# Transposing attention probabilities by an fp32 product with a diagonal of the softmax factors, in place of scaling them in place and transposing

## The chip, the cores and the metric

The kernel runs on one core of one Trainium2 chip. The metric is the device time of one launch in microseconds. Before the change three runs took 1724.89, 1728.59 and 1732.99 us, so the median is 1728.59 us. Everything is float32: one sequence of 256 tokens with 1024 features goes through two blocks of two layers each, and every weight is read from HBM once.

## The reference, cut to what matters

The model holds four mixers with softmax attention. The change touches the softmax of all of them. For one head it is always this, with a causal or banded mask and sometimes a bias, a sink or a gate:

```
def forgetting_attention(q, k, v, f_logit, b_f):        # 8 heads
    logits = einsum('bqhd,bkhd->bhqk', q, k) * scale + c_q - c_k
    p = softmax(where(kpos <= qpos, logits, -inf), axis=-1)
    out = einsum('bhqk,bkhd->bqhd', p, v)

def mla_mixer(...):      # 8 heads:  the same, with rotated parts of q and k
def dilated_mixer(...):  # 12 heads in three groups of patterns; the softmax runs over the three together:
    o, lse = banded_attention(...)             # per pattern
    wts = softmax(stack(lses), axis=0); out = sum(wts * stack(outs))
def swa_mixer(...):      # 8 heads, a sink column in the softmax
def nsa_mixer(...):      # 8 heads, two attentions each (selected blocks, window), each times its own gate:
    out = gate[0] * o_cmp + gate[1] * o_slc + gate[2] * o_win
```

With e = exp(logits - max) the kernel computes p = e * f, where f is 1 / sum(e) for each query (times the gate where there is one). Queries lie on the partitions, so f is one number per partition. The product with v needs p with the keys on the partitions, so p must be transposed.

## The kernel before, in words

The program is one stream of stages over one core: input projections, mixers, output products and feed-forward networks, most of whose time is split-precision products (each float32 weight is split into a high and a low part by ScalarE and VectorE, lines 339 and 347, and TensorE makes three products of the parts, lines 718 to 720, and 939 and 940). The attentions run between an input projection and the output product of their layer, and the output product's parts are interleaved with them.

The class `Attention` (line 1171) writes one attention. The 256 queries are two tiles of 128 (t = 0, 1). A unit is one head; for t = 0 it needs 128 keys and for t = 1 all 256, so its probabilities are 384 columns on 128 partitions, in one of `homes`. Two units (j = 0, 1) make a duo; G duos make a pair m, over which the softmax factor is shared. G is 1 everywhere but in the dilated mixer, where it is 3. The attentions are: fox, 4 duos; mla, 4 duos; dilated, 2 pairs of 3 duos; and the last layer's (sliding window with sinks and the two branches of nsa), 12 duos. That makes 26 duos and 22 pairs. mla and dilated are chained by `Chain` (line 2693), the second starting 4 steps after the first, so that some steps hold work of both.

The order of work is written out by hand, step by step, and every engine executes its own queue in order. In step i:

- TensorE (`tensor`) makes `flips(d, 0)` of an earlier duo d, the `scores` of duo i, a half part of the output product in some steps, `flips(d, 1)`, the `values` of the duo flipped one step before, and the other half part. With G = 1 the duo flipped in step i is i - 2.
- VectorE (`vector`) copies the flip of j = 0 out of PSUM (line 1358), makes the factors of pair i - 1 where G is 1 (line 1352: a reciprocal of the row sums), then adds the bias to the scores of duo i and takes the negative row maxima (line 1326).
- ScalarE (`scalar`) copies the flip of j = 1 out of PSUM (line 1405) and makes the exponentials with their row sums (line 1397).
- GpSimd (`scale`, line 1430) waits for the factors, multiplies them by the gate where there is one (line 1425), and multiplies the probabilities in place, in 128x128 for t = 0 and 128x256 for t = 1, with one count of `pool_a` per unit.

`flips(d, j)` (line 1268) waits for GpSimd's count of its own unit and for the copy that empties the bank of the flip before it: all flips of an attention go through one PSUM bank. It then transposes three blocks of 128x128, `pe.transpose` with the identity as the moving operand (line 1274). The copies go to a ring of four duos, from which `values` (line 1294) multiplies with v. `add_bias` may overwrite a home of probabilities only after its flip (`probs_flipped`).

Of the kernel before, what the change touches and what calls it, by code (L numbers as in the profile page):

```python
# [10 lines left out]
ALU = mybir.AluOpType  # L11
# [1159 lines left out]
class Attention:  # L1171
# [3 lines left out]


    def __init__(self, k, ctx, pairs, first_tile, base=None, banks=(4, 5, 6, 7), started=(), values_in=None,
                 homes=None):
        self.k, self.pairs, self.first_tile = k, pairs, first_tile
        self.base = base or (lambda tile: None)  # L1180
        self.banks, self.started, self.values_in = banks, started, values_in
        self.at = Begun(k)
        self.M, self.G = len(pairs), len(pairs[0]["units"])
        self.duos = self.M * self.G
        self.LAG = 2 if self.G == 1 else 3
        self.DEPTH = len(homes) if homes else 8 if self.G == 1 else 12
        self.RING_T = 4
        self.steps = self.flip_step(self.duos - 1) + 3
        M, G = self.M, self.G

        def sb(name, shape):
            return ctx.enter_context(k.nc.sbuf_tensor(f"att{k.uid()}_{name}", shape, F32))

        if homes is None:
            probs = sb("probs", [P, self.DEPTH, 3 * P])
            homes = [probs[:, n, :] for n in range(self.DEPTH)]
        self.homes = homes
        self.probs_T = k.spare[:].rearrange("p r n -> p (r n)").rearrange("p (r j n) -> p r j n", r=self.RING_T, j=2)
        self.nmax_u, self.rows = sb("nmax_u", [P, M, 2, TT, G]), sb("rows", [P, M, 2, TT, G])
        self.nmax, self.den, self.fac, self.esink = (sb(n, [P, M, 2, TT]) for n in ("nmax", "den", "fac", "esink"))  # L1200

    def flip_step(self, d):

# [42 lines left out]
    def tensor(self, pe, i, between=None):  # L1246

        k = self.k

        def scores(d):  # L1250
            if d == 0:
                for mark in self.started:
                    pe.wait_ge(*mark)
            if d >= 1:
                pe.wait_ge(*self.at.logits_ready.after(2 * d))
            for t in range(TT):
                keys = P * (t + 1)
                for j in range(2):
                    x, out = self.unit(d, j), self.scores_bank(j)[:, self.spots(t)]
                    right = x["tiles"][:, 0:t + 1] if "tiles" in x else x["kT"][:, 0:keys]  # L1260
                    ins = pe.matmul(out, x["q"](t), right, start=True, stop="extra" not in x)  # L1261
                for j in range(2):
                    x, out = self.unit(d, j), self.scores_bank(j)[:, self.spots(t)]
                    for lhsT, rhs in x.get("extra", ()):
                        ins = pe.matmul(out, lhsT, rhs[:, 0:keys], start=False, stop=rhs is x["extra"][-1][1])
            ins.then_inc(self.at.scores_ready.sem, 1)

        def flips(d, j):
            n = 2 * d + j
            pe.wait_ge(*self.at.pool_a.after(n + 1))  # L1270
            if n >= 1:
                pe.wait_ge(*(self.at.probs_T_ready.after(d + 1) if j else self.at.act_a.after(d)))
            for c in range(3):
                ins = pe.transpose(self.flip_bank()[:, P * c:P * c + P], self.probs(n)[:, P * c:P * c + P],  # L1274
                                   k.ident[:])
            ins.then_inc(self.at.probs_flipped.sem, 1)

        def values(d):
            pair = self.pairs[d // self.G]
            tile = pair["tile"]  # L1280
            if d == 0 and self.values_in:
                pe.wait_ge(*self.values_in)
            opens = pair["first"] and d % self.G == 0
            if opens:
                if tile >= 1:
                    pe.wait_ge(*self.at.heads_done.after(tile))
                if self.base(tile):
                    pe.matmul(self.mixed(tile), *self.base(tile), start=True, stop=False, skip_group_check=True)
                    opens = False
            pe.wait_ge(*self.at.probs_T_ready.after(d + 1))  # L1290
            pe.wait_ge(*self.at.act_a.after(d + 1))
            for s in range(TT):
                for j in range(2):
                    ins = pe.matmul(self.mixed(tile)[HD * j:HD * j + HD, P * s:S], self.unit(d, j)["v"](s),  # L1294
                                    self.probs_T[:, d % self.RING_T, j, S * s:S + P * s], start=opens and s == 0,
                                    stop=s == 1 and self.closes(d), skip_group_check=True)
            ins.then_inc(self.at.heads_ready.sem, 1)

        d = self.duo_at(i)
        if d >= 0:  # L1300
            flips(d, 0)
        if i < self.duos:
            scores(i)
        if between:
            between()
        if d >= 0:
            flips(d, 1)
        d = self.duo_at(i - 1)
        if d >= 0:
            values(d)  # L1310
# [107 lines left out]
    def scale(self, pool):  # L1418

        k, G = self.k, self.G  # L1420
        for m in range(self.M):
            gate = self.pairs[m].get("gate")
            pool.wait_ge(*self.at.dve_a.after(m + 1))
            if gate is not None:
                k.pool.done(pool, pool.tensor_tensor(self.fac[:, m], self.fac[:, m], gate, ALU.mult))
            for g in range(G):
                for j in range(2):
                    for t in range(TT):
                        x = self.probs(2 * (m * G + g) + j)[:, self.spots(t)]
                        ins = pool.tensor_tensor(x, x, self.fac[:, m, j, t:t + 1].to_broadcast(list(x.shape)), ALU.mult)  # L1430
                    ins.then_inc(self.at.pool_a.sem, 1)

    def passed(self):

        k, duos, M = self.k, self.duos, self.M
        for mark, n in ((k.scores_ready, duos), (k.heads_ready, duos), (k.logits_ready, 2 * duos),
                        (k.probs_flipped, 2 * duos), (k.pool_a, 2 * duos), (k.probs_T_ready, duos), (k.act_a, duos),
                        (k.probs_ready, M), (k.dve_a, M), (k.dve_b, sum(not self.plain(m) for m in range(M)))):
            mark.passed(n)
        tiles = self.pairs[-1]["tile"] + 1  # L1440
        k.act_b.passed(tiles)
        k.heads_done.passed(tiles)
# [1285 lines left out]
def latent_layer(k, block, enter):  # L2728

    with ExitStack() as ctx:  # L2730
        z, bias = k.layer_views((TT, 2720), (12, S))
        ab = Latent(k, ctx, z, bias)
        ab.loads(block, k.acc[0])
        pieces = [("token", lambda t, c=c, n=n: z[:, t, c:c + n], n) for c, n in AB_CUTS]
        mla = Attention(k, ctx, [dict(tile=p, first=True, last=True, units=[(ab.head(2 * p), ab.head(2 * p + 1))])
                                 for p in range(ab.H // 2)], 0, banks=(4, 5, 6, 7),
                        started=(ab.head_placed.after(8),), values_in=ab.copied[-1], homes=ab.homes)
        product(k, block, "ab_in", KD, pieces, enter, scaled=True, side=ab, then=None)
        k.bias_loaded.passed(16)
        heads_out = k.heads_done.after(0)  # L2740
        mla.passed()
        dil = Attention(k, ctx, [dict(tile=p, first=True, last=True, units=[tuple(ab.dilated(4 * g + 2 * p + j)
                                                                                  for j in range(2)) for g in range(3)])
                                 for p in range(2)], NH, banks=(4, 5, 6, 7), started=(k.logits_ready.after(0),),
                        values_in=k.heads_done.after(0), homes=ab.wide_homes)
        out = OutProduct(k, "ab_out", 6)

        def tile_waits(pe, m):
            if m < 4:
                pe.wait_ge(heads_out[0], heads_out[1] + (2 if m < 2 else 4))  # L2750
            else:
                pe.wait_ge(*k.heads_done.after(2))

        attend(k, block, Chain(mla, dil, 4), out, {6: [0], 8: [1], 10: [2], 12: [3]}, {3: 4, 11: 5, 13: 6, 15: 8},
               side=ab, tile_waits=tile_waits)
        dil.passed()
        out.weights(block)
# [473 lines left out]
```

## Time and profile before

| | |
|---|---|
| median of 3 runs | 1728.59 us |
| the profiled execution | 1731.53 us, span 1729.8 us |
| mean granted TensorE clock | 0.973 of full |
| TensorE busy | 1646.2 us (95%), 8997 matmul records |
| VectorE, ScalarE, GpSimd busy | 1125.7, 942.9 and 117.3 us |
| HBM | 281.81 MB read, 164 GB/s over the span |

Durations in the profile are those of single instructions; matmuls are pipelined, so what one costs in a dense run is the distance between starts. The granted clock has two levels, 1.2 and 2.4 GHz (0.5 and 1.0). In a window that mixes them, PEclk is the mean. The attentions lie at about 122 to 158 us (fox), 945 to 1010 us (mla and dilated) and 1463 to 1528 us (the last layer's). The chain of waits names what each moment of the end time rests on; a line that isn't in it had time to spare at that place.

### The profile page before, as it was taken

How to read it: one execution, taken by the hardware profiler on the slowest of the kernel's cores; microseconds unless marked ns; L12 is line 12 of the kernel's file. 1: busy time of each engine (PE TensorE's matmuls, PEld its weight loads, DVE VectorE, ACT ScalarE, POOL GpSimd, SP SyncE). 2: the span in 40 equal slices, each digit the busy share in tenths (PEclk: the TensorE clock that was granted, in tenths of full speed). 3: DMA queues.
4: the chain of work that ended last, by engine and by line, in shares of the span. 5: the costliest groups of instructions: out<-in, count | busy, mean ns of one | idle time of the engine just before them, and what ended most of it. 6: DMA issues, size and time to landing. Idle time of an engine off the chain costs nothing.

```text
span 1729.8 us, 24635 instructions
## 1 busy us (share of the span) xinstructions
PE 1646.2 (95%) x8997; PEld 1384.6 (80%) x8997; DVE 1125.7 (65%) x1784; ACT 942.9 (55%) x1528; POOL 117.3 (7%) x172
## 2 busy tenths in 40 slices
PE   7998999989889998999999789999999998899998
PEld 7886888888678887888877568888888878578887
DVE  5955766677666667766667457666766673667665
ACT  5544655457565545555556555556555554665454
POOL 0601000000000000000003210000000010410000
PEclk9998999999999999999999899999999998999999
DMA  9332455574336554646464026645465673026652
GB/s 331 105 122 98 147 178 186 188 257 136 107 114 203 194 169 146 201 164 218 161 239 147 1 79 213 211 161 198 160 217 164 224 239 130 1 74 219 198 166 97
DMA packets 215698, 283.91 MB, mean 164 GB/s; under 512 B 8264, under 2 KB 151624, under 8 KB 215624
## 3 DMA queue, kind: packets, MB, share of 16 engines
q1 hardware_dynamic: 215624, 282.93, 48.8%
q8 instruction: 46, 0.75, 0.2%
q14 instruction: 28, 0.23, 0.0%
HBM read 281.81 MB, written 1.09 MB: 164 GB/s over the span
## 4 chain that ended last, share of the span: by engine, by line
PE 86%; DVE 7%; ACT 5%; issue 1%; POOL 1%; DMA 0%; ACTq 0%; SPq 0%; DVEq 0%
PE banks L939 28%; PE banks L940 14%; PE banks L718 12%; PE banks L720 12%; PE banks L719 12%; PE banks L1261 1%; DVE ring_lo L347 1%; PE banks L1294 1%; PE banks L1274 1%; ACT ring_hi L339 1%; PE banks L653 1%; PE banks L1622 1%; PE banks L2880 1%; ACT act_both L637 0%; DVE ffn_down_lo L1060 0%
## 5 line engine op out<-in xcount | busy, mean ns | idle before, releaser
L939 PE MATMUL banks<-act_both,ring_hi 128*128 128x512 f32 x2112 | 750.5, 396 | 3.3 <-DVE act_both L592 1.6
L940 PE MATMUL banks<-act_both,ring_lo 128*128 128x256 f32 x2112 | 592.1, 280 | 0.0
L939 PEld LDWEIGHTS banks<-act_both,ring_hi 128*128 128x128 f32 x2112 | 397.1, 188 | 100.7 <-issue 3.9
L940 PEld LDWEIGHTS banks<-act_both,ring_lo 128*128 128x128 f32 x2112 | 397.0, 188 | 5.0
L1055 DVE TENSOR_TENSOR ring_lo<-weight_slots,ring_hi 128x1024 fp32r<-128x1024 f32 x240 | 283.3, 1222 | 62.2 <-ACT ring_hi L1010 61.8
L347 DVE TENSOR_TENSOR ring_lo<-weight_slots,ring_hi 128x1024 fp32r<-128x1024 f32 (+4 forms) x150 | 181.9, 1227 | 97.0 <-ACT ring_hi L339 93.8
L1010 ACT ACTIVATE ring_hi<-weight_slots 128x1024 fp32r<-128x1024 f32 x240 | 239.2, 1044 | 0.8 <-DMA weight_slots<-in_ffn_w 0.7
L1024 ACT ACTIVATE normed<-banks 128x512 f32<-128x512 f32 x132 | 78.9, 598 | 286.3 <-PE banks L940 286.3
L718 PE MATMUL banks<-ffn_down_hi,ffn_hidden_hi 128*128 128x512 f32 x528 | 207.5, 393 | 0.3
L719 PE MATMUL banks<-ffn_down_lo,ffn_hidden_hi 128*128 128x512 f32 x528 | 206.7, 392 | 0.0
L720 PE MATMUL banks<-ffn_down_hi,ffn_hidden_lo 128*128 128x512 f32 x528 | 205.9, 390 | 0.0
L339 ACT ACTIVATE ring_hi<-weight_slots 128x1024 fp32r<-128x1024 f32 (+4 forms) x150 | 145.8, 992 | 91.4 <-PE banks L720 86.0
L1060 DVE TENSOR_TENSOR ffn_down_lo<-weight_slots,ffn_down_hi 128x1024 fp32r<-128x1024 f32 x132 | 160.8, 1218 | 3.1 <-ACT ffn_down_hi L1017 3.1
L718 PE MATMUL banks<-ring_hi,act_both 128*128 128x512 f32 (+3 forms) x360 | 147.3, 409 | 6.4 <-DVE act_both L2240 1.9
L720 PE MATMUL banks<-ring_hi,act_both 128*128 128x512 f32 (+3 forms) x360 | 139.8, 388 | 0.0
L719 PE MATMUL banks<-ring_lo,act_both 128*128 128x512 f32 (+3 forms) x360 | 139.6, 388 | 0.0
L1017 ACT ACTIVATE ffn_down_hi<-weight_slots 128x1024 fp32r<-128x1024 f32 x132 | 137.8, 1044 | 0.0
L1028 ACT ACTIVATE ffn_silu<-normed 128x256 f32<-128x256 f32 x132 | 55.2, 418 | 137.3 <-DVE normed L1077 95.2
L718 PEld LDWEIGHTS banks<-ffn_down_hi,ffn_hidden_hi 128*128 128x128 f32 x528 | 99.1, 188 | 25.5 <-DVE ffn_down_lo L1060 2.9
L720 PEld LDWEIGHTS banks<-ffn_down_hi,ffn_hidden_lo 128*128 128x128 f32 x528 | 99.2, 188 | 22.0
L1074 DVE TENSOR_TENSOR normed<-banks,normed 128x256 f32<-128x256 f32 x88 | 37.3, 424 | 115.1 <-ACT normed L1024 114.4
L719 PEld LDWEIGHTS banks<-ffn_down_lo,ffn_hidden_hi 128*128 128x128 f32 x528 | 99.1, 188 | 15.8
(378 smaller groups left out, 1925.6 us busy)
## 6 DMA issues: line engine op xcount, KB each, us to landing
weight_slots<-in_ffn_w SPq DMA_DIRECT2D x44, 1024.0 KB, 6.4
weight_slots<-in_ffn_w_gate SPq DMA_DIRECT2D x44, 1024.0 KB, 5.4
weight_slots<-in_ffn_w_up SPq DMA_DIRECT2D x44, 1024.0 KB, 8.0
weight_slots<-in_ffn_w_down SPq DMA_DIRECT2D x88, 512.0 KB, 8.4
weight_slots<-in_ffn_w SPq DMA_DIRECT2D x44, 512.0 KB, 8.3
weight_slots<-in_ev_w_in SPq DMA_DIRECT2D x6, 2048.0 KB, 12.8
weight_slots<-in_od_w_in SPq DMA_DIRECT2D x5, 2048.0 KB, 10.6
weight_slots<-in_ab_w_in SPq DMA_DIRECT2D x4, 2048.0 KB, 11.0
```

The lines of the kernel that those rows point to most:

```text
L339: act.activation(self.hi(n), part.raw, ACT.Copy).then_inc(self.part_hi, 1)
L347: dve.tensor_tensor(self.lo(n), part.raw, self.hi(n).bitcast(F32), ALU.subtract).then_inc(self.part_split, 1)
L718: pe.matmul(out, left[0], right[0], start=start, stop=False, **more)
L719: pe.matmul(out, left[0], right[1], start=False, stop=False, **more)
L720: return pe.matmul(out, left[1], right[0], start=False, stop=stop, **more)
L939: pe.matmul(bank, k.hi(n)[:, q, :], k.act_both[:, q], start=q == 0, stop=False, skip_group_check=True)
L940: return pe.matmul(bank[:, 0:S], k.lo(n)[:, q, :], k.act_hi[:, q, :], start=False, stop=q == KD - 1, skip_group_check=True)
L1010: act.activation(k.hi(part(f, u)), k.parts[part(f, u)].raw, ACT.Copy).then_inc(k.part_hi, 1)
L1017: act.activation(dn_hi[:, f % 2], raw_down(f), ACT.Copy).then_inc(k.down_hi.sem, 1)
L1024: act.activation(cross[:, f % 2], ps[:, bank:bank + 2, S:2 * S], ACT.Copy).then_inc(k.cross_copied.sem, 1)
L1055: dve.tensor_tensor(k.lo(n), k.parts[n].raw, k.hi(n).bitcast(F32), ALU.subtract).then_inc(k.part_split, 1)
L1060: dve.tensor_tensor(dn_lo[:, f % 2], raw_down(f), dn_hi[:, f % 2].bitcast(F32), ALU.subtract).then_inc(k.down_split.sem, 1)
```

## The change

The probabilities stay unscaled. GpSimd builds, per pair m, unit j and query tile t, a diagonal matrix of 128x128: the identity times the factors, broadcast along the row. TensorE multiplies each block of probabilities with the diagonal of its query tile by an ordinary fp32 `matmul` (probabilities stationary, diagonal moving) in place of `transpose` with the identity: the result is the scaled transpose. There are two sets of diagonals (m % 2), so GpSimd waits for the flips of pair m - 2 before it writes; the dilated attention uses the storage of mla's, and waits for all of mla's flips. `pool_a` counts two per pair, not two per duo. The row sums (`den`) are now written to the storage of the factors, and the reciprocal is made in place.

```diff
@@ Attention.__init__
-        self.nmax, self.den, self.fac, self.esink = (sb(n, [P, M, 2, TT]) for n in ("nmax", "den", "fac", "esink"))
+        self.nmax, self.fac, self.esink = (sb(n, [P, M, 2, TT]) for n in ("nmax", "fac", "esink"))
+        self.den = self.fac
+        self.diag = sb("diag", [P, 2, 2, TT, P]) if diag is None else diag
+        self.shared = diag is not None
@@ flips
         def flips(d, j):
-            n = 2 * d + j
-            pe.wait_ge(*self.at.pool_a.after(n + 1))
+            n, m = 2 * d + j, d // self.G
+            pe.wait_ge(*self.at.pool_a.after(2 * m + j + 1))
             if n >= 1:
                 pe.wait_ge(*(self.at.probs_T_ready.after(d + 1) if j else self.at.act_a.after(d)))
             for c in range(3):
-                ins = pe.transpose(self.flip_bank()[:, P * c:P * c + P], self.probs(n)[:, P * c:P * c + P],
-                                   k.ident[:])
+                ins = pe.matmul(self.flip_bank()[:, P * c:P * c + P], self.probs(n)[:, P * c:P * c + P],
+                                self.diag[:, m % 2, j, min(c, 1), :], start=True, stop=True, skip_group_check=True)
             ins.then_inc(self.at.probs_flipped.sem, 1)
@@ scale
-            for g in range(G):
-                for j in range(2):
-                    for t in range(TT):
-                        x = self.probs(2 * (m * G + g) + j)[:, self.spots(t)]
-                        ins = pool.tensor_tensor(x, x, self.fac[:, m, j, t:t + 1].to_broadcast(list(x.shape)), ALU.mult)
-                    ins.then_inc(self.at.pool_a.sem, 1)
+            if m >= 2 or self.shared:
+                pool.wait_ge(*self.at.probs_flipped.after(2 * G * max(m - 1, 0)))
+            for j in range(2):
+                for t in range(TT):
+                    ins = pool.tensor_tensor(self.diag[:, m % 2, j, t, :], k.ident[:],
+                                             self.fac[:, m, j, t:t + 1].to_broadcast([P, P]), ALU.mult)
+                ins.then_inc(self.at.pool_a.sem, 1)
@@ passed
-                        (k.probs_flipped, 2 * duos), (k.pool_a, 2 * duos), (k.probs_T_ready, duos), (k.act_a, duos),
+                        (k.probs_flipped, 2 * duos), (k.pool_a, 2 * M), (k.probs_T_ready, duos), (k.act_a, duos),
@@ latent_layer
-                        values_in=k.heads_done.after(0), homes=ab.wide_homes)
+                        values_in=k.heads_done.after(0), homes=ab.wide_homes, diag=mla.diag)
```

## Rows read from the trace of the kernel before

**Rows 1.** Page: span, busy time and share of each engine, chain of waits by engine.
```profile
span 1729.8 us, 24635 instructions
...
PE 1646.2 (95%) x8997; PEld 1384.6 (80%) x8997; DVE 1125.7 (65%) x1784; ACT 942.9 (55%) x1528; POOL 117.3 (7%) x172
...
PE 86%; DVE 7%; ACT 5%; issue 1%; POOL 1%; DMA 0%; ACTq 0%; SPq 0%; DVEq 0%
```

**Rows 2.** Windows (us): busy and count of PE, PEld, DVE, ACT, POOL; PEclk, DMA share, GB/s.
```profile
122.30:158.50 36.20, 34.67 (x165) 24.76 (x166) 14.79 (x51) 16.30 (x46) 8.49 (x16) 0.81 0.01 2
132.50:135.90 3.40, 2.81 (x20) 1.92 (x19) 1.67 (x9) 0.83 (x3) 1.90 (x4) 1.00 0.00 0
135.90:146.20 10.30, 10.21 (x37) 6.97 (x38) 3.10 (x13) 3.43 (x16) 1.90 (x4) 0.50 0.01 2
945.00:1010.00 65.00, 48.94 (x279) 33.66 (x278) 25.64 (x110) 30.96 (x106) 19.84 (x40) 0.84 0.11 34
996.10:999.50 3.40, 3.33 (x15) 2.30 (x16) 0.29 (x2) 1.44 (x2) 3.11 (x7) 0.50 0.00 0
1463.00:1490.80 27.80, 18.28 (x136) 12.93 (x134) 21.40 (x95) 17.16 (x63) 9.84 (x20) 0.88 0.21 72
1490.80:1528.50 37.70, 36.90 (x236) 25.48 (x238) 20.64 (x74) 21.73 (x72) 19.55 (x37) 1.00 0.12 36
```

**Rows 3.** Line 1274 (transposes) in last attention: count, ns min/median/max, first and last start.
```profile
L1274 PE MATMUL banks<-ident,layer x72: 270/273/421, 1469.2 to 1525.4; 128*128 128x128 f32 x72
```

**Rows 4.** Line 1261 (scores), last attention, by form.
```profile
L1261 PE MATMUL banks<-cd_zT x96: 272/376/632, 1463.1 to 1517.4; 64*128 64x128 f32 x48, 64*128 64x256 f32 x48
```

**Rows 5.** Timeline of TensorE: start us, us, line, operands, count.
```profile
919.30 1.03 PE L2454 MATMUL banks<-ident,layer 128*128 128x128 f32 x8
920.09 0.47 PE L718 MATMUL banks<-ring_hi,act_both 128*128 128x512 f32 x1
...
43.10 1.95 PE L1622 MATMUL banks<-layer 128*128 128x128 f32 x16
44.80 0.48 PE L718 MATMUL banks<-ring_hi,act_both 128*128 128x512 f32 x1
...
687.85 0.61 PE L974 MATMUL banks<-diag_rrms,ones 128*128 128x128 f32 x4
```

**Rows 6.** Chain of waits in order of time: start us, us, what.
```profile
135.99 0.87 PE banks L1274 x3
...
143.78 0.64 PE banks L1274 x3
...
147.64 0.33 PE banks L1274 x3
...
950.46 0.98 POOL normed L1430 x2
...
967.15 0.87 PE banks L1274 x3
...
989.02 3.62 ACT ab_flipped L1397 x16
...
1493.87 0.33 PE banks L1274 x3
```

**Rows 7.** Groups by form (busy us, mean ns | idle) and a wait, in windows of the attentions.
```profile
L1430 POOL TENSOR_TENSOR ab_flipped<-ab_flipped,att_fac 128x128 f32<-128x128 f32 x10 | 4.0, 403 | 27.5 <-DVE att_fac L1352 27.5
L1430 POOL TENSOR_TENSOR ab_flipped<-ab_flipped,att_fac 128x256 f32<-128x256 f32 x10 | 6.2, 617 | 0.0
...
PE banks L1274 <- POOL layer L1430: 1.6, 2, 1.0
...
L347 DVE TENSOR_TENSOR ring_lo<-weight_slots,ring_hi 128x1024 fp32r<-128x1024 f32 x6 | 7.3, 1217 | 1.1 <-ACT ring_hi L339 1.1
L347 DVE TENSOR_TENSOR ring_lo<-weight_slots,ring_hi 128x1024 fp32r<-128x1024 f32 x8 | 11.0, 1376 | 3.2 <-ACT ring_hi L339 3.1
```

More of the change, by code:

```diff
@@ L1177, in __init__ @@
     def __init__(self, k, ctx, pairs, first_tile, base=None, banks=(4, 5, 6, 7), started=(), values_in=None,
-                 homes=None):
+                 homes=None, diag=None):
         self.k, self.pairs, self.first_tile = k, pairs, first_tile
```

## The prediction

> **What bounds the kernel now.** I read the page first. TensorE is busy 95% of the span and holds 86% of the chain of waits [rows 1]; whatever lengthens its instruction stream is paid unless it waits at that place for something else. So the question is how full TensorE is where the edited code runs. The windows of those stretches answer it [rows 2]. The last attention (the one with 12 pairs of heads) is solid from 1490.8 on: 36.90 us busy of 37.7, at full clock. The first attention (122.3 to 158.5) is as full, 34.67 of 36.2, but at a mean clock of 0.81. The two chained attentions (945 to 1010) have 48.94 of 65.0 at 0.84, and the start of the last one (1463 to 1490.8) has 18.28 of 27.8, where VectorE with 21.40 is the fuller. GpSimd is busy 8.5, 19.8, 9.8 and 19.6 us in the four and sets the pace in none. I call a flip the three transposes of one head's probabilities into the shared bank. There are 26 pairs of heads, so 52 flips.
>
> **What TensorE pays per flip.** Before, a flip is three records: the last attention has 12 pairs, 12 x 2 x 3 = 72, and the trace has 72 [rows 3]. An fp32 product is not one record but two: the scores of the same 12 pairs are 24 products over 128 keys and 24 over 256, and the trace has 48 and 48 [rows 4]. So a flip goes from three records to six. What a record costs is its pitch, not its duration of about 273 ns, because they are pipelined. Eight transposes start at 919.30 and the next instruction at 920.09, which is 0.10 each; within the run (1.03 - 0.27)/7 is 0.109. Sixteen records of 128x128 fp32 products start at 43.10, the next one at 44.80: 0.106 each, or (1.95 - 0.275)/15 = 0.112 within. Four records with a diagonal as moving operand are (0.61 - 0.274)/3 = 0.112 [rows 5]. I take 0.11 for both kinds: 0.33 us for a flip now, which is what the chain shows for most of them [rows 6], and 0.66 after. Each flip grows by **0.33 us at full clock**, and by 0.66 where the granted clock is 0.5, since there the chain already has 0.64 to 0.87 for three records [rows 6].
>
> The Trainium skill ("TensorE: Matmul & The Clock Gate", Terms, the xbus row) says that transpose mode is 4 times faster for fp32. With the transposes at the 0.11 of the rows, a product by that rule would take 0.44 and a flip grow by 0.99, which makes the sum below 46 x 0.99 = 45.5 us. The trace disagrees: two records of 0.11 per product, a factor of 2. I go by the rows.
>
> **How many flips are on the path.** Of the 52, the chain of waits holds 39: all 8 of the first attention, 14 of 20 in the chained ones, 17 of 24 in the last (16 of them from 1490.86 on, the solid stretch). Seven of the 39 lie at half clock, from the one at 135.99 to the one at 1478.45; [rows 6] has three of these seven and two at full clock. The other 13 lie beside VectorE or ScalarE: while ScalarE works through a group of three pairs (16 exponentials, 3.62 us at a stretch, [rows 6]), or while VectorE's row of work from 1468 to 1490 is the chain. Their 13 x 0.33 = 4.3 us are hidden there; with that cover gone they are paid. Sum: 32 x 0.33 + 7 x 0.66 = 46 x 0.33 = **15.2 us**.
>
> **What GpSimd saves.** It scaled 128x128 and 128x256 at 403 and 617 ns [rows 7], four operations per pair of heads. Now it makes four diagonals of 128x128 per group, whether the group has one pair of heads or three: 88 x 0.40 = 35 us in place of 52 x 0.40 + 52 x 0.62 = 53 us, none of it binding. What binds is its latency to the first flip: 0.98 for two operations before, at 950.46, the only place where the chain runs over it [rows 6]; then 2 x 0.40 = 0.80. That is 0.2 us. TensorE's waits for GpSimd at the start of the last attention are 1.6 us in two places [rows 7], both off the chain; bounds 0 and 1.6, I take 0. In the chained attention with groups of three the second and third pair no longer wait for their own scaling (12 operations now 4), but their flips wait for the copies out of the bank there. VectorE's splitting of weights takes 1376 ns on average in the last attention, where GpSimd is busier, against 1217 in the first [rows 7]; 8 x 0.16 = 1.3 us is the most that could come back, and only in the VectorE-bound part; I take 0.
>
> **The added wait.** GpSimd now waits, from the third group on, until the flips two groups back are done, and for the second chained attention until all flips of the first are. Behind it on GpSimd's queue are only the diagonals. The factors of group m are made one step after the scores of m, behind the copy of group m-1's first flip on VectorE's queue, so flips of m-2 are past; at the join the last flip of the first attention is at 967.15 [rows 6], while the second has no factors before VectorE has taken the maxima and ScalarE the exponentials of six heads. Cost 0; if it did bind, it would be about one flip, 0.66, per group. The denominators written over the factors keep the same instructions: 0. Storage for diagonals moves no transfer: 0; DMA is idle through most of these stretches (share 0.01 in the first, [rows 2]).
>
> **Sum.** +15.2 - 0.2 = **+15.0 us**. The profiled execution took 1731.5 us (span 1729.8 and 1.7 around it), 2.9 above the median of the three runs; so 1746.5 for an execution like that one, and 1728.6 + 15.0 = **1743.6** for the median.
>
> **Rivals.**
> *A, the forecast, 0.58.* TensorE pays its 46 units.
> *B, the clock is partly spared, 0.16.* The clock fell at 135.9 after a stretch of scores, two flips and a short wait, with TensorE 2.81 busy of 3.4 us; it stayed at half for 10.3 us though TensorE was then busy 10.21 [rows 2]. If six full products in place of three transposes keep it up there, that gives back 10.3/2 = 5.1 us and the dearer half of two flips (0.7): +9.2, **1737.8**. With the 3.4 us at 996.1 [rows 2] as well (1.7, and 0.7 for its two flips) it is +6.8, 1735.4. Against it: the idle time there, waits for copies, remains. The solid stretch from 1490.8 holds 16 flips and stays at 1.00. The Trainium skill (same page, Part 4: PE-mode transpose) says that the full clock doesn't engage for transposes; by that rule the products would help here and B's 1737.8 would be the forecast. The trace doesn't decide it: its flips are short beside the products around them.
> *C, faster, 0.04.* The same mechanism in all attentions. Their half-clock time is 36.2 x 0.19 x 2 + 65 x 0.16 x 2 + 27.8 x 0.12 x 2 = 41.2 us, worth 20.6, and with the dearer half of seven flips (2.3) it gives -7.9: **1720.7**. It turns the sign once some 27 of the 41 us are lifted. Most of these stretches begin after TensorE had waited for VectorE, ScalarE or a new stage, which products don't fill.
> *D, half hidden, 0.10.* In the chained attentions the chain alternates flip, copy, flip, and a longer flip could move into the gaps. Only the full stretches then pay: 6 + 16 flips at 0.33 and 2 at 0.66, +8.6, **1737.2**. Against it: a copy waits for the flip's last record, so the alternation lengthens too.
> *E, all exposed, 0.12.* All 52 flips are paid (59 units, 19.5) and one more stretch of 3.4 us falls to half clock (1.7): +21.2, **1749.8**. What speaks for it: later TensorE instructions move against VectorE's splits.
>
> **Numbers.** What a measurement of this kernel can tell from no change is about 0.5%, 8.6 us: slower begins at 1737.2. A, most of E and half each of B and D lie above; same holds the other halves and a tail of A; faster is C. Slower 0.77, same 0.19, faster 0.04. The range, **1734 to 1750**, takes in B, D and E's value; pitches from 0.10 to 0.112 move the sum from 13.8 to 15.5 and lie inside.
>
> **What would show it.** Flips of six records, 312 in all, about 0.66 us each in the chain, with weight loads of about 188 ns as the products' have; TensorE's busy time up by some 17 to 20 us; GpSimd's in the attentions down from 58 to about 40; the stretch that was 1490.8 to 1528.5 longer by 16 x 0.33 = 5.3 us. Wrong if the clock no longer falls near 135.9 (B), if the chained attentions keep their length (D), or if a product takes another number of records than two.

## The result, and the profile after

The changed kernel takes 1738.43 us (median of 6 runs, 1734.19 to 1739.55); the kernel before, run beside it, 1726.74 us (6 runs). The ratio is **1.0056, 95% interval 1.0038 to 1.0074**: slower by 9.7 us by the ratio, 11.7 by the medians. A repeat with 12 runs gave 1.0041 (1.0024 to 1.0057). Both intervals exclude no change; of the prediction's own bound for slower, 0.5%, the first lies above and the repeat below. The forecast was 1743.6 us, +15.0, slower; the range 1734 to 1750 holds the time, but the point is 5.3 us too high by the ratio. Rival B, whose mechanism is a clock that is partly spared, had named 1737.8.

From the page of the changed kernel, as in [rows 1]:

```profile
span 1737.2 us, 24947 instructions
...
PE 1657.9 (95%) x9153; PEld 1402.7 (81%) x9153; DVE 1124.0 (65%) x1784; ACT 942.7 (54%) x1528; POOL 98.6 (6%) x156
...
PE 86%; DVE 7%; ACT 5%; issue 1%; POOL 1%; DMA 0%; ACTq 0%; SPq 0%; DVEq 0%
```

The profiled execution took 1738.93 us. TensorE has 156 more records than in [rows 1] (9153 against 8997), 52 flips x 3, and is busy 11.7 us longer; GpSimd is busy 18.7 us less. The span grew by 7.4. The prediction had TensorE's busy time up by 17 to 20; it missed that, and the last parts say why.

The new line 1277 in the last attention (weight loads, then products; ns min/median/max), to be held against [rows 3]:

```profile
L1277 PEld LDWEIGHTS banks<-att_diag,layer x144: 186/192/337, 1470.9 to 1532.6; 128*128 128x128 f32 x144
L1277 PE MATMUL banks<-att_diag,layer x144: 270/275/527, 1470.9 to 1532.8; 128*128 128x128 f32 x144
```

It has 144 records where the transposes had 72, 275 ns at the median (was 273). Its weight loads take 192. The chain of waits shows what a flip costs now; these answer to [rows 6]:

```profile
137.91 1.62 PE banks L1277 x6
...
146.46 1.28 PE banks L1277 x6
...
150.21 0.67 PE banks L1277 x6
...
952.23 0.77 POOL att_diag L1433 x2
...
970.34 1.50 PE banks L1277 x6
...
1495.93 0.67 PE banks L1277 x6
```

A flip at full clock takes 0.67 us (was 0.33), at half clock 1.28 to 1.62 (was 0.64 to 0.87). GpSimd's first two operations in the chained attentions take 0.77 (were 0.98). The groups of GpSimd, TensorE's wait for it in the last attention, and VectorE's splits there, against [rows 7]:

```profile
L1433 POOL TENSOR_TENSOR att_diag<-ident,att_fac 128x128 f32<-128x128 f32 x88 | 38.3, 467 | 158.1 <-DVE att_fac L1355 157.5
...
PE banks L1277 <- POOL att_diag L1433: 1.2, 1, 1.2
...
L347 DVE TENSOR_TENSOR ring_lo<-weight_slots,ring_hi 128x1024 fp32r<-128x1024 f32 x8 | 9.9, 1242 | 3.3 <-ACT ring_hi L339 3.2
```

The splits fell from 1376 to 1242 ns and the wait from 1.6 to 1.2 us; what that is worth is told below, with the kernel that makes the diagonals and keeps the transposes. The windows of the changed kernel, cut at marks that every kernel has (start of an attention's first scores, start of the residual's transposes behind it); columns as in [rows 2]:

```profile
120.45:175.51 55.06, 48.20 (x242) 36.71 (x241) 24.95 (x65) 24.84 (x58) 6.79 (x16) 0.87 0.22 77
175.51:947.89 772.38, 746.85 (x4035) 634.89 (x4036) 521.45 (x707) 435.53 (x641) 17.84 (x23) 0.99 0.53 177
947.89:1018.26 70.37, 56.27 (x354) 43.16 (x353) 29.15 (x113) 32.58 (x107) 8.85 (x24) 0.95 0.14 46
1018.26:1464.63 446.37, 439.11 (x2322) 374.59 (x2321) 293.03 (x441) 242.60 (x355) 4.53 (x9) 0.98 0.55 181
1464.63:1543.69 79.06, 71.83 (x480) 55.06 (x480) 44.58 (x172) 42.30 (x139) 24.31 (x56) 0.96 0.22 70
```

The part of the last attention in which TensorE is nearly always busy, between the same instructions as the row from 1490.80 to 1528.50 in [rows 2], is 43.4 us long (was 37.7), at full clock both times:

```profile
1492.49:1535.89 43.40, 42.60 (x284) 32.20 (x286) 19.66 (x74) 21.94 (x72) 16.16 (x37) 1.00 0.15 45
```

All kernels below are cut at the same marks. The table is worked out from the start times in the traces; in brackets stands the half-clock time in the stretch, from the record of the granted clock.

| profile | records per flip | first attention | from there to the chained ones | chained attentions | to the last one | last attention | span |
|---|---|---|---|---|---|---|---|
| before | 3 | 52.2 (15.1) | 774.6 (29.3) | 69.8 (20.5) | 447.2 (17.1) | 73.2 (6.8) | 1729.8 |
| before again | 3 | 52.3 (14.7) | 774.8 (29.6) | 66.8 (13.7) | 447.2 (17.1) | 73.2 (6.8) | 1728.2 |
| diagonals, transposes | 3 | 49.2 (9.0) | 774.3 (28.5) | 69.4 (20.5) | 447.1 (17.1) | 72.3 (6.8) | 1726.9 |
| **after** | 6 | 55.1 (14.0) | 772.4 (20.1) | 70.4 (6.8) | 446.4 (13.7) | 79.1 (6.8) | 1737.2 |
| after again | 6 | 50.6 (3.4) | 773.4 (23.9) | 70.2 (6.8) | 446.4 (13.7) | 79.0 (6.8) | 1733.5 |
| identity products | 6 | 53.6 (10.2) | 772.4 (17.1) | 72.2 (13.7) | 448.8 (20.5) | 79.6 (6.8) | 1739.3 |
| transposes twice | 6 | 50.3 (3.4) | 772.9 (23.9) | 71.6 (13.7) | 446.5 (13.7) | 80.3 (13.7) | 1735.1 |
| first only | 6 there | 50.5 (3.4) | 773.6 (23.9) | 69.1 (20.5) | 447.2 (17.1) | 73.2 (6.8) | 1726.9 |
| chained only | 6 there | 52.2 (15.2) | 774.5 (29.2) | 70.6 (6.8) | 446.4 (13.7) | 73.4 (6.8) | 1729.9 |
| last only | 6 there | 49.2 (9.4) | 774.1 (28.2) | 69.2 (20.5) | 444.8 (10.2) | 80.8 (10.2) | 1730.7 |
| burst, first flip | 3 | 53.4 (12.2) | 774.3 (28.7) | 69.4 (20.5) | 444.8 (10.2) | 73.8 (13.7) | 1729.9 |
| burst, last flip | 3 | 52.8 (11.5) | 774.7 (29.5) | 66.8 (13.7) | 447.2 (17.1) | 73.2 (6.8) | 1728.8 |
| longer burst | 3 | 54.1 (12.8) | 775.1 (28.1) | 68.1 (17.1) | 447.2 (17.1) | 73.2 (6.8) | 1731.8 |
| one-row filler | 3 | 57.5 (13.7) | 772.6 (17.1) | 63.6 (3.4) | 447.2 (17.1) | 73.2 (6.8) | 1726.9 |

Two things are to be seen in it. Where half-clock times match, the price of the flips is near the forecast: +2.9 in the first attention (14.0 against 15.1 us at half clock, not quite equal), +4.8 to +5.4 in the chained ones at 13.7 (71.6 and 72.2 against 66.8 twice), +5.8 in the last at 6.8, and +6.3 there with identity products (79.57 against 73.25). And part is given back: the stretch behind the first attention, in which the kernels don't differ at all, is 1.2 to 2.2 us shorter, and in the changed kernel's two profiles the chained attentions have 6.8 us at half clock, where the two of the kernel before have 20.5 and 13.7.

### The profile page after: what moved, and what is told of

Read it like the earlier page. It is cut to its first block, busy times and chain, and to the rows that moved or that the text cites. A ratio compares the mean times of both kernels' runs of the same rounds, so it can differ in the third digit from the quotient of the medians.

```text
span 1737.2 us, 24947 instructions
## 1 busy us (share of the span) xinstructions
PE 1657.9 (95%) x9153; PEld 1402.7 (81%) x9153; DVE 1124.0 (65%) x1784; ACT 942.7 (54%) x1528; POOL 98.6 (6%) x156
## 4 chain that ended last, share of the span: by engine, by line
PE 86%; DVE 7%; ACT 5%; issue 1%; POOL 1%; DMA 0%; ACTq 0%; SPq 0%; DVEq 0%
PE banks L939 28%; PE banks L940 14%; PE banks L718 12%; PE banks L719 11%; PE banks L720 11%; PE banks L1277 2%; DVE ring_lo L347 1%; PE banks L1264 1%; PE banks L1297 1%; ACT ring_hi L339 1%; PE banks L653 1%; PE banks L1626 1%; PE banks L2884 1%; ACT act_both L637 0%; DVE ffn_down_lo L1060 0%
## 5 line engine op out<-in xcount | busy, mean ns | idle before, releaser
L718 PE MATMUL banks<-ring_hi,act_both 128*128 128x512 f32 (+3 forms) x360 | 145.0, 403 | 6.4 <-DVE act_both L2244 1.9
L720 PE MATMUL banks<-ring_hi,act_both 128*128 128x512 f32 (+3 forms) x360 | 138.5, 385 | 0.0
```

The lines of the kernel that those rows point to most:

```text
L718: pe.matmul(out, left[0], right[0], start=start, stop=False, **more)
L720: return pe.matmul(out, left[1], right[0], start=False, stop=stop, **more)
```

## The experiments

Each was timed beside the kernel before. The mean granted clock is over all runs of a kernel; for before it was 0.975.

**The kernel before again.** No edit.

> The kernel before, unchanged. In the profiles of before and after, the mean granted clock was 0.973 and 0.982 of full, and the stretch at half clock that began at 965.4 lasted 13.7 us before and 3.4 us (from 970.9) after. Theory W (the products keep TensorE's clock up): the runs of before keep a mean clock of about 0.973 and the profile again has some 10 us at half clock between 965 and 985. Rival P (phase: where the clock falls and for how long differs from run to run of one kernel): the runs spread over 0.973 to 0.982 or so, and this profile need not have the long stretch. Ratio to before 1.000 within 0.3%.

1730.30 us over 12 runs, ratio 1.0011 (0.9997 to 1.0025), mean clock 0.9745, runs 0.973 to 0.976. Windows of its first attention, of the stretch behind it and of the chained ones:

```profile
120.42:172.72 52.30, 45.44 (x217) 32.81 (x217) 24.89 (x65) 24.84 (x58) 8.50 (x16) 0.86 0.23 81
172.72:947.49 774.77, 749.82 (x4034) 637.85 (x4035) 521.52 (x707) 435.57 (x641) 18.80 (x23) 0.98 0.52 176
947.49:1014.28 66.79, 50.51 (x295) 34.92 (x293) 29.27 (x113) 32.58 (x107) 19.83 (x40) 0.90 0.15 48
```

The half-clock stretch in the chained attentions is 10.2 us here (from 966.9), 13.7 us in all. So its length does vary from run to run, and 3 us of the chained attentions with it (69.8 and 66.8). But none of its 12 runs, nor of the 24 of before beside them, has a mean clock above 0.978, where the changed kernel's six have 0.982 to 0.984. Beside the later kernels 4 of 77 runs of before reach 0.982 to 0.984; they took 1717.43, 1717.87, 1720.52 and 1723.91 us. Theory P explains the spread, not the difference.

These four also give the price without the clock's part. The eighteen runs of the changed kernel have 0.981 to 0.984 and took 1734.2 to 1739.6 us. On the one chip on which both kernels had a run at 0.984, the changed one took 1735.23 and the one before 1720.52: +14.7 us at an equal mean clock, where the forecast was +15.0. It is a single pair; it is the nearest that the record has to the forecast's own terms.

**Identity products, GpSimd as before.**

```diff
-                ins = pe.transpose(self.flip_bank()[:, P * c:P * c + P], self.probs(n)[:, P * c:P * c + P],
-                                   k.ident[:])
+                ins = pe.matmul(self.flip_bank()[:, P * c:P * c + P], self.probs(n)[:, P * c:P * c + P],
+                                k.ident[:], start=True, stop=True, skip_group_check=True)
```

> The kernel before with one edit: flips are fp32 products with the identity in place of transposes; GpSimd scales the probabilities in place as before. Theory T (all of the price is TensorE's six records per flip): flips of about 0.66 us in place of 0.33, ratio to before like the change's, 1.0056 to 1.0065 (+10 to +11 us), since GpSimd's part is worth 0.2 us. Rival G (GpSimd's lighter work hides part of the price in the change): without it the price is the full +15 us, 1.0087.

1739.53 us over 6 runs, ratio 1.0056 (1.0039 to 1.0074), mean clock 0.982. The same ratio as the change: the price is TensorE's, and rival G, which had 1.0087 here, falls. Its windows behind the first attention and of the chained ones:

```profile
172.97:945.32 772.35, 746.66 (x4034) 634.03 (x4035) 521.35 (x707) 435.69 (x641) 17.82 (x23) 0.99 0.52 177
945.32:1017.50 72.18, 57.89 (x355) 43.66 (x354) 29.42 (x113) 32.58 (x107) 19.84 (x40) 0.91 0.14 44
```

**Diagonals made, transposes kept.** In the changed kernel:

```diff
-                ins = pe.matmul(self.flip_bank()[:, P * c:P * c + P], self.probs(n)[:, P * c:P * c + P],
-                                self.diag[:, m % 2, j, min(c, 1), :], start=True, stop=True, skip_group_check=True)
+                ins = pe.transpose(self.flip_bank()[:, P * c:P * c + P], self.probs(n)[:, P * c:P * c + P],
+                                   k.ident[:])
```

> The changed kernel with transposes with the identity in place of its products: GpSimd makes the diagonals and all waits are the change's, but nothing multiplies with the diagonals, so this kernel leaves the scaling of the probabilities out. Theory T: GpSimd's part alone is worth nothing that can be measured, -0.2 us, ratio 0.9999 (0.998 to 1.002). Rival G: -3 to -5 us, 0.997 to 0.998, from VectorE's and GpSimd's shorter work in the attentions.

1727.55 us over 12 runs, ratio 0.9992 (0.9978 to 1.0005), mean clock 0.977. By the times GpSimd's part is worth -1.4 us with an interval that reaches from -3.8 to +0.9: nothing that can be told from none. GpSimd's group shows that the added wait did hold it once here:

```profile
L1433 POOL TENSOR_TENSOR att_diag<-ident,att_fac 128x128 f32<-128x128 f32 x88 | 38.2, 466 | 153.5 <-DVE att_fac L1355 148.3 <-PE banks L1277 4.6
```

4.6 us of GpSimd's idle time, in one wait in the last attention, ended with TensorE's flips of two groups back.

The profile does show a gain where the times can't. The last attention, here and (second line) in the kernel before:

```profile
1459.27:1531.58 72.31, 63.21 (x407) 44.70 (x407) 44.25 (x172) 42.44 (x139) 24.26 (x56) 0.95 0.21 72
...
1463.08:1536.33 73.25, 62.93 (x407) 44.50 (x407) 46.06 (x172) 42.43 (x139) 29.39 (x56) 0.95 0.21 71
```

It is 0.9 us shorter, with VectorE busy 1.8 us less, at the same 6.8 us of half clock; six profiles with three records per flip and GpSimd's scaling have 73.2 there, all of them. The gain lies before the flip that opens the full stretch: 26.8 us from the first scores to that flip (1459.27 to 1486.11), where the kernel before has 27.8 (1463.08 to 1490.86). Identity products with GpSimd's old scaling and the changed kernel differ the same way, by 0.5 us (28.4 and 27.9). So GpSimd's lighter work does shorten the part that VectorE bounds. That the two engines hinder each other there is argued from VectorE's shorter splits and not shown by itself.

**Every transpose twice.** In the kernel before:

```diff
-                ins = pe.transpose(self.flip_bank()[:, P * c:P * c + P], self.probs(n)[:, P * c:P * c + P],
-                                   k.ident[:])
+                for again in range(2):
+                    ins = pe.transpose(self.flip_bank()[:, P * c:P * c + P], self.probs(n)[:, P * c:P * c + P],
+                                       k.ident[:])
```

> The kernel before with each transpose issued twice: six records per flip as in the change, but all in transpose mode, GpSimd's part as before. Theory T: the price is that of records, about 0.11 us each, so the same time as the identity products within 0.2%. Theory W (products count for the clock and transposes don't): the mean clock stays at before's 0.973 while the identity products have about 0.982, and this kernel is 5 to 7 us slower than they are.

1737.56 us over 7 runs, ratio 1.0047 (1.0030 to 1.0063), mean clock 0.980. Its line in the last attention, then two of its windows (behind the first attention, chained):

```profile
L1275 PEld LDWEIGHTS banks<-ident,layer x144: 137/141/230, 1467.7 to 1530.5; 128*128 128x128 f32 x144
...
L1275 PE MATMUL banks<-ident,layer x144: 270/273/444, 1467.7 to 1530.6; 128*128 128x128 f32 x144
...
170.38:943.24 772.86, 747.73 (x4034) 635.75 (x4035) 521.24 (x707) 435.67 (x641) 18.87 (x23) 0.98 0.53 177
...
943.24:1014.80 71.56, 57.10 (x355) 41.69 (x354) 29.23 (x113) 32.59 (x107) 19.88 (x40) 0.90 0.14 45
```

144 transpose records cost what 144 product records do, though their weight loads take 141 ns and not 192, and the clock rises as well. Theory W falls: it isn't products against transposes, it is six records against three.

**Identity products in one attention at a time** (first, chained, last), each by a condition on the edit above.

```diff
+                if self.banks == (6, 7, 4, 5):        # chained: (4, 5, 6, 7); last: self.M == 12
+                    ins = pe.matmul(...)
+                else:
+                    ins = pe.transpose(...)
```

> The kernel before with identity products in the first attention only (8 flips). Marks so far: from the first scores of the first attention to the residual's transposes after it 52.2 us before (15.1 at half clock), 55.1 after; from there to the chained attentions, where the kernels don't differ, 774.6 before and 774.8 and 774.3 in two other kernels with three records per flip, but 772.4, 772.4 and 772.9 with six. Theory S (a longer first attention moves the later stages against the points at which the clock can change, and so half-clock time goes): the stretch after it is 772.4 to 772.9 here too, the first attention costs +2.5 to +3.7, the total is +0.5 to +1.5 us, ratio 1.0003 to 1.0009. Rival N (that was chance in three profiles): 774.6 again, +3 us, 1.0018.

First only: 1727.58 us over 12 runs, ratio 0.9992 (0.9973 to 1.0011), mean clock 0.9795. Windows of the first attention and of the stretch behind it:

```profile
119.67:170.21 50.54, 43.69 (x241) 33.37 (x241) 25.04 (x65) 24.83 (x58) 8.49 (x16) 0.97 0.24 84
170.21:943.77 773.56, 748.03 (x4034) 635.28 (x4035) 520.98 (x707) 435.45 (x641) 18.86 (x23) 0.98 0.52 176
```

The eight longer flips cost nothing in sum that could be measured. The attention is at half clock for 3.4 us only, and 1 us comes back behind it (773.6, less than the 1.7 to 2.2 that theory S named).

> The kernel before with identity products in the two chained attentions only (20 flips, 14 on the chain of waits). Theory T with S: the first attention and the stretch after it as before (52, 774.6); the chained attentions 67 to 70 before, plus 14 x 0.33 + some at half clock, less what half clock goes: +2 to +5; total ratio 1.0012 to 1.003. Rival D (flips there mostly hidden beside ScalarE and VectorE): under +1 us, 1.0005.

Chained only: 1732.58 us over 12 runs, ratio 1.0029 (1.0011 to 1.0048), mean clock 0.978. Its chained attentions, 70.6 us with 6.8 at half clock:

```profile
946.04:1016.59 70.55, 56.25 (x355) 43.18 (x354) 29.33 (x113) 32.58 (x107) 19.84 (x40) 0.95 0.14 46
```

> The kernel before with identity products in the last attention only (24 flips, 17 on the chain of waits). Theory T: that attention goes from 73.2 to 79.1 us as in the changed kernel, +5.9, and nothing else moves: ratio 1.0034 (1.003 to 1.004). Rival: part of it comes back as clock in the stages after it, 1.002.

Last only: 1735.32 us over 12 runs, ratio 1.0035 (1.0014 to 1.0057), mean clock 0.976. Its last attention:

```profile
1456.41:1537.22 80.81, 73.92 (x480) 56.57 (x480) 46.45 (x172) 42.30 (x139) 29.39 (x56) 0.94 0.21 69
```

Here the attention is 80.8 with 10.2 at half clock, against 73.2 with 6.8; the ratio gives 0.0035 x 1729 = 6.1. The three ratios add to 1.0056 (-0.8 + 2.9 + 3.5 per thousand), which is the ratio of the whole. Each has an interval of about 2 per thousand to either side, so that the sum is met so closely is luck.

**A burst in one place.** The first flip of the first attention nine times, 24 more transposes:

```diff
-            for c in range(3):
+            again = 9 if self.banks == (6, 7, 4, 5) and n == 0 else 1     # late: 7 or 11, n == 7
+            for c in [c for _ in range(again) for c in range(3)]:
```

> The kernel before with the first flip of the first attention issued nine times (24 more transposes, 24 x 0.11 = 2.6 us, at one place), everything else as before. Theory S (the shift alone matters, not the kind or the place of the work): the first attention +2.6, the stretch after it 772.4 to 772.9, total 0 to +1 us, ratio 1.0000 to 1.0006, mean clock above before's 0.975. Rival A (flips spread over the attention keep the clock up by their activity): the stretch after it stays 774.6 and the total is +2.6, 1.0015.

1729.36 us over 12 runs, ratio 1.0006 (0.9987 to 1.0025), mean clock 0.976. The stretch behind it stays at 774.3 us. As many records as in the first-only kernel, at one place, save nothing behind it: theory S falls in this form. I then formed theory L, that only a delay behind the attention's half-clock stretch counts, and put the burst at the last flip.

> The kernel before with the last flip of the first attention issued seven times (18 more transposes, 18 x 0.11 = 2.0 us). The burst at the first flip left the later stages alone (774.3 to the chained attentions). Theory L (the place where the half-clock stretch of the first attention ends sets the timing of what follows; only work behind it moves the later stages against the points at which the clock changes, and the four flips behind it in the changed kernel do that): the stretch after the first attention falls from 774.6 to about 772.5, the half-clock stretch at its start (6.8 us from about 170) to 3.4, and the total stays at 0 to +0.3 us, ratio 1.0000. Rival A (longer flips spread over the attention, by their activity, are what saves half-clock time): 774.3, total +2.0 us, 1.0012.

1730.56 us over 12 runs, ratio 1.0014 (0.9995 to 1.0033), mean clock 0.977. The first attention and the stretch behind it:

```profile
120.60:173.36 52.76, 45.91 (x235) 34.00 (x235) 24.88 (x65) 24.83 (x58) 8.48 (x16) 0.89 0.23 80
173.36:948.07 774.71, 749.76 (x4035) 637.60 (x4036) 521.60 (x707) 435.47 (x641) 18.81 (x23) 0.98 0.52 176
```

> The same with the last flip issued eleven times (30 more transposes, 3.3 us). Theory L: the place of the clock's changes repeats, and this much later they lie as in the kernel before: the stretch after it is 774.3 to 774.8 again, with 6.8 us at half clock at its start, and all of the delay is paid: +3.3 us, 1.0019. Rival (more work in front of the idle time always saves half-clock time there): 772.5 or less, total +1 us, 1.0006.

1733.66 us over 12 runs, ratio 1.0014 (0.9994 to 1.0034), mean clock 0.975; 54.1 and 775.1 us. L named 772.5 for the first of the two and it is 774.7. The longer one is about as L had it (774.3 to 774.8 named), but a theory that misses the one and hits the other, where the rival A's value for the first is met, isn't borne out.

**The changed kernel again.** No edit.

> The changed kernel again. Theory T with L: ratio 1.0056 to 1.0068 (+10 to +12 us), mean clock 0.981 to 0.984; the first attention about 50 to 55 us long, the stretch after it 772.4 to 772.9, the last attention 79 to 80.

1736.22 us over 12 runs, ratio 1.0041 (1.0024 to 1.0057), mean clock 0.982, every run between 0.981 and 0.984. The ratio is below the expected 1.0056; the intervals overlap. The stretch behind the first attention is 773.4, above the expected 772.9. The two profiles of this one kernel differ most in the first attention: 55.1 us with 14.0 at half clock in the one, 50.6 with 3.4 in the other, which has no fall of the clock near 135.9 at all.

**A filler one row deep.** In the kernel before, ahead of each flip of the first attention:

```diff
+            if self.banks == (6, 7, 4, 5):
+                pe.matmul(self.flip_bank()[:, 0:S], k.ones[0:1, 0:P], k.ones[0:1, 0:S], start=True, stop=True,
+                          skip_group_check=True)
             for c in range(3):
```

> The kernel before with one more fp32 product ahead of each of the 8 flips of the first attention, one row deep (2 records of 256 columns, about 0.3 us, as long as the 0.33 us that the products add); the flips stay transposes. It fills TensorE's time as products in the first attention alone do (50.5 us with 3.4 at half clock, 773.6 us to the chained attentions, mean clock 0.9795 over 12 runs, ratio 0.9992), but with hardly any work in the array. Theory R (it is the spread of the delay over the attention, whatever fills it): the same as that kernel, mean clock 0.979 to 0.980, 772.4 to 773.6 after it, ratio 0.999 to 1.000. Theory A (it is what the array does in that time): mean clock 0.975 as before, half-clock time in the first attention 7 to 15 us, 774.3 to 775.1 after it, and +2.5 to +4 us, ratio 1.0015 to 1.0023.

1736.18 us over 9 runs, ratio 1.0049 (1.0031 to 1.0068). Eight of the nine runs have a mean clock of 0.972 to 0.975; the profiled one is the ninth, at 0.982 and 1728.69 us. Its first filler and flip, and its three windows:

```profile
132.21 0.69 PE L1274 MATMUL banks<-ones 1*128 1x256 f32 x2
...
132.84 0.55 PE L1277 MATMUL banks<-ident,att_probs 128*128 128x128 f32 x3
...
119.31:176.85 57.54, 50.69 (x233) 34.32 (x232) 24.95 (x65) 24.84 (x58) 8.50 (x16) 0.88 0.21 74
...
176.85:949.47 772.62, 746.93 (x4035) 634.17 (x4036) 521.52 (x707) 435.64 (x641) 18.88 (x23) 0.99 0.53 177
...
949.47:1013.06 63.59, 47.29 (x294) 32.95 (x293) 29.27 (x113) 32.58 (x107) 19.85 (x40) 0.97 0.16 51
```

The filler took 0.63 us, not 0.3, so the attention grew by 5.3 us and the ratio can't be held against the first-only kernel's. The clock can: it doesn't rise to 0.979 as theory R had it, but stays at or below before's in all runs but one. That speaks for A, though a filler of twice the intended length isn't the same delay. The ninth run is against a plain A: the same instructions, at 0.982, with 772.6 us behind the first attention and 3.4 us at half clock in the chained ones, where nothing was edited.

## Why the prediction was right, and where it was off

The direction and the terms of TensorE's sum were right. That the range holds the time is partly luck: it had been drawn wide enough to take in B and D, and the measured price is 9.7 us where the sum said 15.0.

**Two records per product, 0.11 each: right.** 312 records, 0.67 us a flip. Twice the transposes cost what the products cost (ratios 1.0047 and 1.0056, with intervals that overlap), and their kernel's mean clock rose like the products' did, to 0.980 from 0.975. The Trainium skill ("TensorE: Matmul & The Clock Gate") has a factor of 4 for fp32 in transpose mode (Terms); the runs show 2. The Trainium skill also has, on the same page, that the full clock doesn't engage for transposes (Part 4: PE-mode transpose); these runs speak against it, by that rise and by the 0.33 us of a transposed flip at full clock against 0.64 at half.

**Which flips are on the path: right in sum.** Forecast by parts: 3.3 in the first attention, 5.9 less 0.2 in the chained ones (14 flips, four at half clock), 5.9 in the last. Measured at equal or nearly equal half-clock times: 2.9, 4.8 to 5.4 and 5.8 to 6.3, together 13.5 to 14.6 against 15.0. In the last attention two small misses cancel. The full stretch grew by 5.7 where 16 x 0.33 = 5.3 was forecast. Ahead of it identity products need 28.4 us (1466.27 to 1494.67), 0.6 more than the 27.8 of the kernel before and as forecast (0.66 for one flip at half clock), but the changed kernel needs 27.9 (1464.63 to 1492.55): its lighter work for GpSimd gives 0.5 back. The other 13 flips didn't all stay hidden either: the changed kernel's chain of waits holds 42 flips where 39 were counted (8, 16 and 18 in the three places). E, in which all 52 are paid, falls all the same. D, in which the chained attentions hide theirs, seems to be met at first sight, since they kept their length (69.8 and 70.4 us), which the prediction had named as its sign; but that was the clock, 20.5 against 6.8 us at half. Identity products in these attentions alone cost 1.0029, where D named 1.0005.

**GpSimd and the added wait: the size was off.** 0.77 in place of 0.98 at the one place on the chain, as forecast. The prediction put the relief of VectorE's splits at 0 of at most 1.3 us; it was worth 0.5 beside the products and 0.9 beside the transposes, too little for the time to show. The diagonals take 467 ns on average, not the 0.40 us that I took: 38.3 us in place of 35, and GpSimd is on the chain nowhere else.

**The clock: the step that failed.** Case A took over the half-clock stretches of the trace of before. By the mean clocks of many runs, the kernel before has (1 - 0.975) x 2 x 1729 = 86 us at half clock and the changed one (1 - 0.982) x 2 x 1737 = 63. That is 23 us less, worth 11 us at most and about 4 by what the time shows (14 less 9.7); this 4 is an estimate by difference. TensorE's busy time, which rose by 11.7 and not by 17 to 20, goes with it: in the stretch behind the first attention, with the same records, it fell from 749.6 us in the kernel before to 746.9 (the row from 175.51 above):

```profile
171.53:946.12 774.59, 749.60 (x4035) 637.38 (x4035) 521.38 (x707) 435.58 (x641) 18.80 (x23) 0.98 0.52 176
```

The pair of runs at an equal mean clock, +14.7, says the same from another side.

Rival B had the mechanism and nearly the time. Its place is met in one of the changed kernel's two profiles and not in the other: the profile of the result still has its 10.2 us from 137.6 on, the repeat has none there (nor have transposes twice and first only). In the profile of the result the saving came at the chained attentions (20.5 to 6.8 us), where of the prediction's cases only C put some, and outside the attentions (29.3 to 20.1, and 17.1 to 13.7), where none did.

**What stays open.** It is shown that six records per flip raise the mean clock, by products or by transposes; in the first attention alone they raise it to 0.9795, in the chained ones alone to 0.978, in the last alone hardly (0.976). It is shown that the same number of records at one place, or a filler one row deep, doesn't, in nearly all runs. Whether it is what the array does during those flips or where they leave the following stages in time is not settled: each theory fits some of the profiles and one misses in each.

No kernel of these beats the kernel before beyond its interval; the nearest, identity products in the first attention and diagonals without products (which leaves the scaling out), are at 0.9992.

## What to carry to other kernels

Where TensorE is the bound, an operand that is scaled on its way through a transpose isn't free: an fp32 product has twice the records of an fp32 transpose, and taking work from an engine that is idle most of the time (GpSimd, 7%) pays little back: here 0.5 to 0.9 us in the one part that VectorE bounds. Count records by the flips that the chain of waits holds, and check the count at equal half-clock time. Put the clock in the range and not in the point: between profiles of one and the same kernel it moved one stage by 3 us here, more than half of what the edit cost there, and another by 4.5. Where both kernels have runs at the same mean clock, compare those too.

## What the runs showed that I had not expected

- A longer chain can be free: eight flips lengthened by 0.33 us each in the first attention left the time at 0.9992 (0.9973 to 1.0011); its profile has 3.4 us at half clock there, before's 15.1.
- Products one row deep over 256 columns took 0.63 us for two records at full clock, against 0.67 for six records of 128x128.
- The same instruction stream ran at mean clocks of 0.972 and 0.982, 1736 and 1728.7 us.
